# A decoder block with attention, mLSTM and a routed mixture of experts: a rebuilt end, expert items of at most 224 rows, and five late V projections

## The reference

```python
h = rms_norm(x, norm_attn_g)
proj = h @ w_in                       # 1024 x 3080: q, k, v of group A; q|k, v, o, gates of group B
a = diff_attention(...)               # 4 heads, T5 bias, causal
m = mlstm_chunkwise(...)              # 4 heads, after a causal convolution of q|k
x = x + concat(head_norm(a), head_norm(m) * o_gate) @ w_out
h2 = rms_norm(x, norm_ffn_g)
top_val, top_idx = top_k(h2 @ router_w + router_b, 4)     # 4 of 32 experts a row
gates = softmax(top_val)
for e in experts:                     # for the rows that chose e
    gu = h2[rows] @ w_gu[e] + b_gu[e]                     # 1024 x 2048
    act = min(gu[:, :1024], 7) * sigmoid(1.702 * glu) * (clip(gu[:, 1024:], -7, 7) + 1)
    y[rows] += gates * (act @ w_down[e] + b_down[e])      # 1024 x 1024
return rms_norm(x + y, final_norm_g)
```

## Time and profile before

| | us |
|---|---|
| runs, median (lowest to highest of 3) | 2373.15 (2372.42 to 2374.28) |
| the profiled execution | 2369.1 |
| its span, first to last instruction | 2367.3 |
| TensorE busy | 2304.7 (97%) |
| DVE, ACT, POOL busy | 774.3, 606.5, 257.1 |
| granted TensorE clock, mean | 0.99 of full speed |

### The profile page before, as it was taken

How to read it: one execution, slowest core, us unless ns; L and a number is a source line. 1 busy time by engine, 2 the same in 40 slices (tenths; PEclk the granted TensorE clock), 3 DMA queues, 4 the chain that set the end, 5 groups by cost and what they waited for, 6 DMA issues and landing times.

```text
span 2367.3 us, 41329 instructions
## 1 busy us (share of the span) xinstructions
PE 2304.7 (97%) x15445; PEld 1984.7 (84%) x15447; DVE 774.3 (33%) x1839; ACT 606.5 (26%) x1276; POOL 257.1 (11%) x235
## 2 busy tenths in 40 slices
PE   7999999999989999999999999999999999999995
PEld 4444554566579999999999999989999999999995
DVE  3342222677652223222222223312222232222225
ACT  2123121344312222222222222212222222222222
POOL 1000000021230001001100001000000000001002
PEclk9999999999999999999999999999999999999998
DMA  8000001210168899989999799966977788798787
GB/s 295 35 1 0 0 16 56 90 61 28 64 217 256 273 293 297 283 279 295 283 286 292 217 283 298 306 194 194 293 237 219 229 275 246 237 286 281 220 252 257
DMA packets 441065, 486.66 MB, mean 206 GB/s; under 512 B 24536, under 2 KB 417928, under 8 KB 440988
## 3 DMA queue, kind: packets, MB, share of 16 engines
q1 hardware_dynamic: 420140, 450.33, 57.7%
q0 software_dynamic: 20656, 35.56, 7.1%
q10 hardware_dynamic: 224, 0.16, 0.0%
HBM read 475.54 MB, written 49.58 MB: 222 GB/s over the span
## 4 chain that ended last, share of the span: by engine, by line
PE 95%; issue 1%; DVE 1%; ACT 1%; DMA 1%; POOL 0%; SPq 0%; DVEq 0%; POOLq 0%
PE PS L1043 66%; PE PS L649 14%; PE PS L845 5%; PE PS L978 2%; PE PS L936 2%; PE PS L818 1%; PE PS L785 1%; PE PS L807 1%; PE PS L730 0%; PE PS L727 0%; PE PS L864 0%; DVE unit L1521 0%; PE PS L685 0%; PE PS L622 0%; PE PS L959 0%
## 5 line engine op out<-in xcount | busy, mean ns | idle before, releaser
L1043 PE MATMUL PS<-pairA,unit 128*128 x12288 | 1576.1, 291 | 5.1 <-issue 4.1
L1043 PEld LDWEIGHTS PS<-pairA,unit 128*128 128x128 f32 x12288 | 1553.4, 190 | 21.3 <-issue 10.0
L649 PE MATMUL PS<-pairA,unit 128*128 128x512 f32 (+1 forms) x528 | 233.1, 597 | 2.3 <-issue 2.3
L1296 ACT ACTIVATE unit<-PS,cur_b 128x256 f32<-128x256 f32 x256 | 107.5, 471 | 454.7 <-PE PS L1043 454.7
L1784 DVE TENSOR_SCALAR unit<-PS,cur_b 128x256 f32<-128x256 f32 x256 | 112.0, 479 | 337.0 <-PE PS L1043 336.8
L545 POOL DMA_INDIRECT unit<-h_dram,cur_x x66 | 68.6, 1040 | 1279.7 <-DVE cur_x L1780 1197.2
L649 PEld LDWEIGHTS PS<-pairA,unit 128*128 128x128 f32 (+1 forms) x528 | 97.9, 189 | 119.9 <-issue 119.3
L1283 ACT ACTIVATE unit<-unit 128x512 f32<-128x512 f32 x128 | 80.7, 631 | 445.4 <-DVE unit L1784 445.4
L1287 ACT ACTIVATE unit<-PS,cur_b 128x256 f32<-128x256 f32 x256 | 107.5, 471 | 316.2 <-PE PS L1043 316.2
L1791 DVE TENSOR_SCALAR unit<-unit 128x512 f32<-128x512 f32 x128 | 54.7, 427 | 339.6 <-ACT unit L1287 339.4
L1773 DVE COPY cur_b<-b_all 128x24 f32 x32 | 6.7, 208 | 437.6 <-ACT unit L1296 433.7
(11 more groups left out here) (253 smaller groups left out, 1261.9 us busy)
## 6 DMA issues: line engine op xcount, KB each, us to landing
unit<-in_expert_w_gu_dram SPq DMA_DIRECT2D x256, 1024.0 KB, 5.2
unit<-in_expert_w_down_dram SPq DMA_DIRECT2D x128, 1024.0 KB, 6.6
unit<-in_w_in_dram SPq DMA_DIRECT2D x6, 2048.0 KB, 15.3
pairB<-in_x_dram SPq DMA_DIRECT2D x16, 512.0 KB, 6.6
unit<-in_w_out_dram SPq DMA_DIRECT2D x2, 2048.0 KB, 9.3
h_dram<-pairA SPq DMA_DIRECT2D x8, 512.0 KB, 2.6
acc_dram<-pairB SPq DMA_DIRECT2D x8, 512.0 KB, 3.5
pairB<-acc_dram SPq DMA_DIRECT2D x8, 512.0 KB, 6.4
```

Of the source, the lines that this page charges most:

```text
L649: ins = pe.matmul(ps, lhs, rhs, start=(k == 0), stop=(k == KD - 1))
L1043: ins = pe.matmul(bank(s)[:, ITEM * j:ITEM * j + w], slot_w[s][:, k, P * j:P * j + P], xa_cols[:, ITEM * k:ITEM * k + KD * ITEM + w][:, ba ...
L1296: ins = act.activation(yT[:, 2 * s + j, :], bank(s)[:, ITEM * j:ITEM * j + ITEM], ACT.Identity, bias=cur_b[:, 2 * NF + 2 * s + j:2 * NF + ...
```

## The change

The expert items hold at most `CAP` = 224 rows: the widest pass is 224 columns, the lists have room for five items of an expert, the planner has a fourth round, and `slots` splits a place into item and row by a multiplication and a shift. Five projections of V in place of four are late; chunk 3 of the mLSTM has two projections, and the first late one stands ahead of the first logits. Two means of the first rows (tiles 2 and 3) are made one step earlier. ACT's loop starts with the evacuations of the down pass of the item before; the first item's gate and up part stands ahead of the loop, and the last item's evacuations behind it. At the end SP skips the loop over extra items when there are none, the tiles go in the order 0, 2, 1, 4, 3, 5, 6, 7, ACT squares tiles 1, 3, 5, 6 and 7 between its last evacuations, eight output buffers take the place of three, the last products are turned and added in two sides, and the two halves of the last rows have their own means and powers.

The core of the diff (where blocks of the old end are removed, only the new lines stand; the moved body of `gate_up` is cut):

```diff
 ITEM = 256
-LISTS = SEQ // P
-MAX_EXTRA = 15
+CAP = 224
+MAX_EXTRA = 18
 ITEMS = N_EXP + MAX_EXTRA
 GROUP = 8
-ROUNDS = SEQ // ITEM - 1
-WIDTHS = [132, 148, 168, 184, ITEM]
+ROUNDS = (SEQ - 1) // CAP
+LISTS = 2 * (ROUNDS + 1)
+CAP_BITS = 21
+CAP_MUL = (1 << CAP_BITS) // CAP + 1
+WIDTHS = [132, 148, 168, 184, CAP]
...
-        DVE_TILES = 5
-        out_sb = kn(unit[1][:, 1024:4096], 3)
+        out_sb = [unit[1][:, 1024 * i:1024 * i + 1024] for i in range(1, 4)]
+        out_sb += [unit[2][:, 1024 * i:1024 * i + 1024] for i in range(4)] + [unit[3][:, 2112:3136]]
+        TAIL_ORDER = (0, 2, 1, 4, 3, 5, 6, 7)
+        ACT_SQUARES = ((1,), (3, 5), (6, 7), ())
+        act_count = {t: n + 1 for n, t in enumerate(sum(ACT_SQUARES, ()))}
...
+        x_idx = unit[3][:, 3136:3136 + N_EXP * LISTS].bitcast(I32)
...
-        LATE_V = 4
+        LATE_V = 5
         shared, chunk_outs = [], []
         for t in range(NT):
-            o = first_shared + (3 * t if t < 4 else 2 * t + 4)
-            chunk_outs.append(range(o, o + (3 if t < 4 else 2)))
+            o = first_shared + (3 * t if t < 3 else 2 * t + 3)
+            chunk_outs.append(range(o, o + (3 if t < 3 else 2)))
...
-            with sp.Fori(N_EXP, ITEMS) as i:
-                with sp.If(i < last):
-                    item_weights(i, sp.value_load(item_e[0:1, bass.ds(i, 1)], min_val=0, max_val=N_EXP - 1))
+            with sp.If(last > N_EXP):
+                with sp.Fori(N_EXP, ITEMS) as i:
+                    with sp.If(i < last):
+                        item_weights(i, sp.value_load(item_e[0:1, bass.ds(i, 1)], min_val=0, max_val=N_EXP - 1))
 
             sp.wait_ge(y_sent, last + 1)
-            for t in range(NT):
+            for t in TAIL_ORDER:
                 sp.dma_start(acc[:, t, :], acc_dram[P * t:P * t + P, :]).then_inc(rows_in[t], 16)
-            for t in range(NT):
-                sp.wait_ge(out_ready, t + 1)
-                sp.dma_start(out_rows[t], out_sb[:, t % 3, :]).then_inc(out_sent[t % 3], 16)
-            for i in range(3):
-                sp.wait_ge(out_sent[i], 16 * len(range(i, NT, 3)))
+            for n, t in enumerate(TAIL_ORDER):
+                sp.wait_ge(out_ready, n + 1)
+                sp.dma_start(out_rows[t], out_sb[t]).then_inc(out_sent, 16)
+            sp.wait_ge(out_sent, 16 * NT)
...
-            step.do(pool.memset(x_idx[:, :], NO_ROW))
-            pool.dma_start(list_dram.rearrange("(p c) o -> p (c o)", p=P), x_idx[:, :]).then_inc(list_clear, 16)
+            step.do(pool.memset(no_rows[:, :], NO_ROW))
+            for half in range(2):
+                pool.dma_start(list_dram.rearrange("(p c) o -> p (c o)", p=P)[:, 160 * half:160 * half + 160],
+                               no_rows[:, :]).then_inc(list_clear, 16)
...
-            for t in range(NT):
-                pool.wait_ge(mean_sq, 3 * NT + t + 1)
+            for n, t in enumerate(TAIL_ORDER):
+                pool.wait_ge(mean_sq, 3 * NT + n + 1)
                 pool.tensor_tensor(rstd[:, t:t + 1], ssq[:, t:t + 1], neg_half[:, 0:1],
                                    ALU.pow).then_inc(rstd_ready, 1)
-            pool.wait_ge(mean_sq, 4 * NT + 1)
-            pool.tensor_tensor(small[:, 4:6], small[:, 0:2], neg_half[:, 0:2], ALU.pow).then_inc(rstd_ready, 1)
-            for i in range(3):
-                pool.wait_ge(out_sent[i], 16 * len(range(i, NT, 3)))
+            for b in range(2):
+                pool.wait_ge(mean_sq, 4 * NT + b + 1)
+                pool.tensor_tensor(small[:, 4 + b:5 + b], small[:, b:b + 1], neg_half[:, 0:1],
+                                   ALU.pow).then_inc(rstd_ready, 1)
+            pool.wait_ge(out_sent, 16 * NT)
...
+            pe.wait_ge(ml_c_ready, NT - 1)
+            late_values(0)
             da_logit(0)
-            late_values(0)
+            late_values(1)
             da_logit(1)
-            late_values(1)
+            late_values(2)
             for u in range(2, N_UNITS + 2):
                 t = u // 4 - 2
                 da_turn_weights(u - 2, 0)
...
                     ml_turn(NT - 1, next_bank("ml", NT - 1))
                 if u < N_UNITS:
                     da_logit(u)
-                if u < LATE_V:
-                    late_values(u)
+                if u + 1 < LATE_V:
+                    late_values(u + 1)
...
             def turn_last():
                 pe.wait_ge(rhs_ready, 8 * last + 4)
-                for s in range(SLOTS):
-                    pe.wait_ge(bank_read[s], 48 * last + 16)
-                turn_y()
+                for side in range(2):
+                    for s in (2 * side, 2 * side + 1):
+                        pe.wait_ge(bank_read[s], 48 * last + 16)
+                    for q in (side, side + 2):
+                        for m in range(4):
+                            ins = pe.transpose(bank(4 + q)[:, P * m:P * m + P],
+                                               yT[:, 4 * side + m, P * (q // 2):P * (q // 2) + P], ident[:, :])
+                        ins.then_inc(y_ps, 1)
...
-                            one_pass([ITEM])
+                            one_pass([CAP])
...
+                if u == 0:
+                    take_out(N_OUTS - LATE_V)
...
+            def gate_up(i):
+                act.wait_ge(cur_b_ready, i + 1)
...
+            def take_down(s, passes):
+                act.wait_ge(slab_done[s], passes)
+                for j in range(2):
+                    ins = act.activation(yT[:, 2 * s + j, :], bank(s)[:, ITEM * j:ITEM * j + ITEM], ACT.Identity,
+                                         bias=cur_b[:, 2 * NF + 2 * s + j:2 * NF + 2 * s + j + 1])
+                ins.then_inc(bank_read[s], 16)
+            gate_up(0)
             act.wait_ge(items_ready, 2)
             last = act.value_load(n_items[0:1, 0:1], min_val=N_EXP, max_val=ITEMS)
             item = act.alloc_register("act_item")
-            act.reg_mov(item, 0)
+            act.reg_mov(item, 1)
...
-                                ins.then_inc(bank_read[s], 16)
+                                take_down(s, 3 * i)
+                            gate_up(i)
...
+            for s in range(SLOTS):
+                take_down(s, 3 * last)
+                for t in ACT_SQUARES[s]:
+                    act.wait_ge(rows_in[t], 32)
+                    if act_count[t] > 1:
+                        act.wait_ge(sum_squared, act_count[t] - 1)
+                    act.activation(sum_squares[:, 1, :], acc[:, t, :], ACT.Square,
+                                   accum_out=ssq[:, t:t + 1]).then_inc(sum_squared, 1)
             for b in range(2):
                 act.wait_ge(last_summed, 2 * b + 2)
+                act.wait_ge(sum_squared, len(act_count) + b)
...
+                if t < 2:
+                    mean_square(t + 2)
...
-                if t + 2 < NT:
+                if 2 <= t < NT - 2:
...
-                step.do(dve.tensor_copy(slot_i[:, t, :], slot[:, t, :]))
-                dve.tensor_scalar(slot_lo[:, t, :], slot_i[:, t, :], P - 1, 8, ALU.bitwise_and, ALU.logical_shift_left)
-                step.do(dve.tensor_scalar(slot_hi[:, t, :], slot_i[:, t, :], 7, None, ALU.logical_shift_right))
-                step.do(dve.tensor_tensor(slot[:, t, :], slot_hi[:, t, :], slot_lo[:, t, :], ALU.add))
+                step.do(dve.tensor_scalar(slot_i[:, t, :], slot[:, t, :], float(CAP_MUL), None, ALU.mult))
+                step.do(dve.tensor_scalar(slot_hi[:, t, :], slot_i[:, t, :], CAP_BITS, None, ALU.logical_shift_right))
+                step.do(dve.scalar_tensor_tensor(out=slot[:, t, :], in0=slot_hi[:, t, :], scalar=float(-CAP), in1=slot[:, t, :],
+                                                 op0=ALU.mult, op1=ALU.add))
+                row_part = small[:, 24:28]
+                step.do(dve.tensor_scalar(row_part, slot[:, t, :], float(P), float(1 - P * N_EXP * LISTS), ALU.is_ge, ALU.mult))
+                step.do(dve.scalar_tensor_tensor(out=slot[:, t, :], in0=slot[:, t, :], scalar=float(N_EXP * LISTS),
+                                                 in1=row_part, op0=ALU.mult, op1=ALU.add))
+                step.do(dve.scalar_tensor_tensor(out=slot[:, t, :], in0=slot_hi[:, t, :], scalar=2.0, in1=slot[:, t, :],
+                                                 op0=ALU.mult, op1=ALU.add))
...
-            dve.tensor_scalar(item_e[0:1, extra], item_col[0:1, extra], 3, None, ALU.logical_shift_right)
+            step.do(dve.tensor_scalar(item_e[0:1, extra], item_col[0:1, extra], 3, None, ALU.logical_shift_right))
+            step.do(dve.tensor_scalar(item_col[0:1, extra], item_col[0:1, extra], 7, 1, ALU.bitwise_and,
+                                      ALU.logical_shift_left))
+            step.do(dve.scalar_tensor_tensor(out=item_col[0:1, extra], in0=item_e[0:1, extra], scalar=float(LISTS),
+                                             in1=item_col[0:1, extra], op0=ALU.mult, op1=ALU.add))
...
+            def add_last(q):
```

(37 more changed lines are left out.)

92 lines of the change are left out of this document (29 added, 63 removed).

## The result

| | before | after |
|---|---|---|
| runs, median (lowest to highest), us | 2372.78 (2368.37 to 2374.28, 4 runs) | 2354.37 (2353.94 to 2355.13, 4 runs) |
| the profiled execution; its span, us | 2369.1; 2367.3 | 2353.94; 2352.1 |
| TensorE, DVE, ACT busy, us | 2304.7, 774.3, 606.5 | 2296.8, 778.8, 566.2 |

A forecast was written before the change was run, and what follows sets the result against it. Bound: TensorE's matmuls, the experts' being 66% of the span. Terms -10.2 - 9.1 - 0.8 = -20.1 us took 2369.1 to 2349.0; with the median 4.05 us higher, 2353 us, range 2347 to 2361 for 8 in 10.

The forecast's parts named there:

- items of 224 rows: Widest expert item: three passes of 24.22 us instead of 27.63, 3.41 us less each, nothing late behind them: -10.2 us.
- the end: After the last weight slab: tile reads issued sooner, two tiles' squares moved from DVE to ACT: -9.1 us, bounds -11.2 and -4.4.
- late V projections: Ahead of the first logits in attention: TensorE's 0.78 us wait for ACT goes: -0.8 us, bounds 0 and -0.8.
- means of tiles 2 and 3: At the start: scales come earlier but the first projection starts as before: 0 us, bounds 0 and a 1.06 us loss.
- slots, planner: Routing and lists: extra DVE steps are covered by other waits and work: 0 us; without cover 7.6 us lost.
- a 33rd item: Rival: the widest item has over 224 rows, so another item costs 75 us, giving 2428 us; chance 0.02.
- 2328.8: At the end: time in us when the first tile lands and DVE starts, after reads issued at about 2324.
- the walk: At the end: ACT's and DVE's steps timed one by one; DVE runs 2328.8 to 2350.2, scatter at 2351.0, 9.1 us sooner.
- Squares that hold back evacuations: Rival: at the end, ACT's squares delay its last evacuations; the end gains 4.4 us or less, 2357.8 to 2362; chance 0.14.
- Code elsewhere: Rival: shifted instruction blocks add or remove one TensorE stall of 4.4 to 5.0 us, 2348 or 2358; chance 0.09.
- ACT's new loop: Rival: loop turn and table load stall TensorE in each item, 31 us per us beyond 9.9 spare; chance 0.05.
- The median's step: The runs' median lies 4.05 us above the profiled execution, so 2349.0 us became a forecast of 2353.

The follow-up runs named there:

- e1_items: Kernel before with only the items of at most 224 rows (constants, lists, slots, planner): 2361.16 us, ratio 0.9964.
- e2_end: Kernel before with only the rebuilt end (SP's skipped loop, tile order, ACT's squares, eight output buffers, sums and powers by half): 2365.04 us, ratio 0.9978.
- e6_evac: Changed kernel with ACT's squares regrouped: tile 5 after evacuation 2, tiles 6 and 7 after evacuation 3: 2352.83 us, ratio 0.9916.
- e12_both: Changed kernel with items of at most 218 rows and ACT's squares of tiles 5, 6 and 7 moved behind later evacuations: 2350.55 us, ratio 0.9910.
- e10_noskip: Kernel before with the rebuilt end but without SP's skipped loop over extra items: 2369.59 us, ratio 0.9987.
- e5_again: Changed kernel run and traced once more, no edit: 2354.23 us, ratio 0.9920.
- e7_218: Changed kernel with items of at most 218 rows in place of 224: 2352.44 us, ratio 0.9912.
- e8_skip: Kernel before with one edit: SP enters the loop over extra items only if there are any: 2365.74 us, ratio 0.9973.
- e9_208: Changed kernel with items of at most 208 rows, so the longest list needs a 33rd item: 2429.79 us, ratio 1.0242.
- e11_planner: Changed kernel with the planner's first operation on 2304 elements done five times instead of once: 2359.89 us, ratio 0.9947.

## Why the prediction was right, and where it was off

The terms, as the traces without a fall of the clock give them:

| term | forecast | measured |
|---|---|---|
| items of 224 rows | -10.2 | -10.2 (3 x 3.41); by the runs of e1_items -8.5 (-5.7 to -11.4) |
| the end | -9.1 | -8.1 (59.85 - 51.78, four and five traces); by the runs of e2_end -5.2 (-3.3 to -7.4) |
| late V projections | -0.8 | -0.6 |
| means of tiles 2 and 3 | 0 | not to be told from 0 |
| slots, planner | 0 | 0 (e1_items), with cover for 5.9 us more |
| sum | -20.1 | -18.9; by the medians of the runs -18.4 and -18.1, by the ratios -16.8 and -19.0 |

The parts by their runs come to less than the whole; the intervals are wide and the clock differs from run to run, and where the difference goes is open.

*Items.* Every step held: the length by columns (also at 218 and 208, 23.57 and 22.51 us), the 217 or 218 rows read from the size of a gather, and that nothing is late behind a shorter pass. The rival of a 33rd item was real as a danger and priced too low: 75 us forecast, 77 measured with passes 1.7 us shorter, as the empty rounds of TensorE's loop were left out.

*The end, the step that was mis-sized.* "At about 2324" for the reads was right; "2328.8" for the first landing was not. Behind the start of the last item's second pass the first square was put at 20.9 us and comes at 21.8 to 23.0 in the five traces with this end (mean 22.3). From there on the walk was right as a sum: 29.4 us from the first square to the end of the span, forecast (2367.3 - 9.1 - 2328.8) and measured (mean of five). But that it came out to the tenth is luck, two errors against each other: in the first trace the last output is ready 0.8 us sooner behind the first square than I had it, and the scatter comes 0.6 us later behind that output. The 3.55 us that the sum took for this landing were misread: in the earlier trace rows the scatter waits for DVE's last norms (L1846), not for an output. e6_evac and e12_both, where it again waits for DVE, have 3.58 us there; in the five traces where it does wait for the landing it is 4.1 to 4.5 us. The first tile's landing was worked out as if its bytes were the next to move once the slabs are in. But in the last 2.7 us ahead of the first square two tiles' worth of rows moved, all on SP's queue (q1):

```profile
DMA packets 311, 1.08 MB, mean 399 GB/s; under 512 B 31, under 2 KB 54, under 8 KB 311
...
q1 hardware_dynamic: 311, 1.08, 100.3%
```

A tile is 0.52 MB. The kernel before shows the same, with no slab in the way: from the issue of its reads to its first square (2331.4 to 2335.1 us) this queue moved 1.7 tiles:

```profile
q1 hardware_dynamic: 232, 0.88, 70.0%
```

The rate was not the fault: 399 GB/s here, against the 420 of the earlier trace rows that the sum used. The Trainium skill's page that the prediction weighed (DMA: Bandwidth & Descriptors, "Where 436 GB/s comes from") has the HBM side bind at about 358 GB/s for transfers between HBM and SBUF. The 399 lie above that, and the measurement decides. In both traces, then, the first of eight reads that are queued together is complete only when about two tiles have moved, and so it lands late; that this comes from shares of the 16 engines that run apart is my reading, and wasn't tried by itself.

*What the end's gain hangs on.* The forecast costed the end as a whole. The traces split it: 6.9 us for a loop of SP that does nothing and 1.1 for all the rest, or 6.1 and 2.0 when the loop goes last.

*Rivals.* Squares that hold back evacuations: they do, by 3.8 us in the change (the last slab's matmuls end at 2330.4, its evacuation starts at 2334.17) and 8.9 us in e10_noskip, and DVE, which has tiles to norm until then, waits in neither, as argued. Code elsewhere: the stalls at 693 and 1322 us stayed at 5.13 and 4.82 us. ACT's new loop: no pass waits for ACT, and instead of one table load an item (32 of them, 1.28 us each, before) there is one in all; ACT's busy time fell by 40 us, which buys nothing, since it wasn't the bound.

*Late V.* The wait at the first logits went, as forecast; that 0.2 us of the 0.8 come back at a later wait for ACT lies within the stated bounds.

*The median's step.* I added 4.05 us to the profiled execution before, as its median lay above it. That was right for the medians, and the 15.2 us between the two profiled executions mislead: before's trace is one of its fastest (2369.1, where its 29 runs beside the first experiments have a median of 2371.67), after's one with half clock in routing.

## What to carry to other kernels

Before rebuilding a tail, look at the queue engine's own chain: a loop that does nothing (15 rounds of 0.5 us) was worth three to six times the reordering of everything behind it. When matmul time is proportional to columns, set the limit of an item from the longest list that the trace shows, and know the price of one row too many (here 77 us against 10). Split a difference of two traces by stage and take a second trace of the same program before explaining any stage: two of this program differed by 5.5 us.

## What was not expected of the hardware

The granted clock fell to half for several us in an unbroken stretch of projections, with TensorE busy all the time, in six of fourteen traces, at about 153 us (e5_again, e7_218, e8_skip, e9_208, e10_noskip, e11_planner; a projection of up to 10.1 us instead of 7.06), and not in others of the same code. The runs follow it: the kernel before has a mean span of 2367.9 us in 11 runs with a mean clock of 0.990 and of 2373.1 in 3 runs with 0.986. Its 29 runs there spread from 2368.8 to 2377.0 us. So two single runs don't tell a difference of a few us, and a stretch at half clock in one trace says nothing by itself about the code there.

Empty rounds of a loop with a condition in it cost 0.5 us each on SP (15 of them in 7.4 us before) and 0.73 on TensorE (17 of them in 12.5 us in e9_208).
